# Routers in TensorE's column groups, and an earlier start of three mixture-of-experts stages

## The reference

```python
def moe_swiglu(u, router_w, w1, w3, w2):            # "MoE 1" here
    logits = (tokens @ router_w).astype(F32)        # 256 x 1024 by 1024 x 8
    top_vals, top_idx = lax.top_k(logits, TOP_K)
    gates = jax.nn.softmax(top_vals, axis=-1)
    ...                                             # tokens sorted by expert
    return (jax.nn.silu(xb @ w1[e]) * (xb @ w3[e])) @ w2[e]

def grouped_moe(x, router_w, router_b, w_gate, w_up, w_down):   # "MoE A", "MoE B"
    scores = jax.nn.sigmoid(xt @ router_w)          # 1024 x 16
    sel = scores + router_b
    group_score = lax.top_k(sel.reshape(-1, N_GROUPS, GROUP_SIZE), TOP_K)[0].sum(-1)
    top_group = jnp.argmax(group_score, axis=-1)
    _, idx = lax.top_k(jnp.where(in_group, sel, -jnp.inf), TOP_K)
    gate = gate / gate.sum(-1, keepdims=True)
    for e in range(N_EXPERTS_2):
        h = jax.nn.silu(xt @ w_gate[e]) * (xt @ w_up[e])
        out = out + combine[:, e:e + 1] * (h @ w_down[e])
```

## Time and profile before

| | |
|---|---|
| median of three runs | 2630.08 us |
| the profiled execution's own time | 2639.58 us |
| its span | 2637.7 us |
| TensorE busy | 2414.2 us (92%) |
| VectorE, ScalarE busy | 479.3 us, 358.8 us |
| mean DMA rate | 243 GB/s |

### The profile page before, as it was taken

The page is one execution under the profiler, slowest core; times in us unless marked ns, Lnnn a source line. Parts: engine busy times, 40 slices in busy tenths (PEclk is TensorE's granted clock), DMA queues, the critical chain, the costliest instruction groups (busy, mean ns, idle before and its releaser), DMA issues. The chain is left out here.

```text
span 2637.7 us, 34623 instructions
## 1 busy us (share of the span) xinstructions
PE 2414.2 (92%) x15312; PEld 1056.6 (40%) x15312; DVE 479.3 (18%) x1109; ACT 358.8 (14%) x847; POOL 33.5 (1%) x77
## 2 busy tenths in 40 slices
PE   4997877999899899999999999987899989789997
PEld 2574653444576433222222223254432228442222
DVE  2133342000248400000000000113100021210002
ACT  2013221000232110000000000021100011110000
POOL 2000000000000000000000000000000000000000
PEclk9998668999999899999999999987799999789999
DMA  8222145542463489999999999921799972359994
GB/s 282 96 96 96 64 168 194 192 160 100 167 248 141 153 292 322 366 367 365 363 365 365 365 366 364 326 82 61 250 360 365 365 283 80 113 195 364 364 360 154
DMA packets 446102, 644.54 MB, mean 244 GB/s; under 512 B 10723, under 2 KB 345019, under 8 KB 445947
## 3 DMA queue, kind: packets, MB, share of 16 engines
q1 hardware_dynamic: 442011, 629.55, 69.5%
q0 software_dynamic: 3936, 12.69, 1.5%
HBM read 641.15 MB, written 1.05 MB: 243 GB/s over the span
## 5 line engine op out<-in xcount | busy, mean ns | idle before, releaser
L1024 PE MATMUL bank<-ring,wide 128*32 128x512 f32 x7296 | 809.8, 596 | 2.6 <-issue 1.7
L1024 PEld LDWEIGHTS bank<-ring,wide 128*32 128x32 f32 x7296 | 231.5, 110 | 551.2 <-issue 551.2
L1052 PE MATMUL bank<-dreg,RB 128*32 128x512 f32 x3648 | 415.0, 595 | 0.0
L1582 ACT ACTIVATE SG<-bank 128x256 f32<-128x256 f32 x114 | 43.7, 384 | 1194.5 <-PE bank L1024 1194.5
L1052 PEld LDWEIGHTS bank<-dreg,RB 128*32 128x32 f32 x3648 | 106.9, 109 | 223.7 <-issue 223.7
L697 PE MATMUL bank<-wide,ring 128*128 128x256 f32 x832 | 180.9, 379 | 0.0
L697 PEld LDWEIGHTS bank<-wide,ring 128*128 128x128 f32 x832 | 158.1, 190 | 22.6 <-issue 1.4
L953 PE MATMUL bank<-ring,wide 128*128 128x512 f32 x352 | 156.9, 600 | 6.5 <-DMA ring<-in_l_ffn_w 6.5
L2282 DVE TENSOR_TENSOR H<-SG,bank 128x256 f32<-128x256 f32 x66 | 27.8, 421 | 722.7 <-ACT SG L1582 722.7
L687 PE MATMUL bank<-ring,wide 128*128 128x512 f32 x352 | 156.7, 605 | 2.3 <-DMA ring<-in_w_kv 2.3
L687 PE MATMUL bank<-ring,T 128*128 128x512 f32 x256 | 114.3, 607 | 1.4 <-ACT sm L1749 0.8
(11 more groups left out here) (371 smaller groups left out, 1466.4 us busy)
## 6 DMA issues: line engine op xcount, KB each, us to landing
ring<-in_l_moe_w SPq DMA_DIRECT2D x176, 1024.0 KB, 11.5
dreg<-in_l_moe_w SPq DMA_DIRECT2D x88, 1024.0 KB, 12.3
ring<-in_w_gate SPq DMA_DIRECT2D x64, 1024.0 KB, 11.3
ring<-in_w_up SPq DMA_DIRECT2D x64, 1024.0 KB, 13.5
dreg<-in_w_down SPq DMA_DIRECT2D x64, 1024.0 KB, 12.4
ring<-in_l_mod_w SPq DMA_DIRECT2D x24, 2048.0 KB, 8.0
ring<-in_l_ffn_w SPq DMA_DIRECT2D x22, 1024.0 KB, 10.3
ring<-in_l_w_in SPq DMA_DIRECT2D x7, 2048.0 KB, 9.0
```

What stands on the lines that cost most here:

```text
L1024: mm = pe.matmul(banks[r % 2][32 * g:32 * g + 32, :], xg[:, k, at:at + 32], ring[:, i % RING, k, :], start=k == 0, stop=k == KC - 1)
L1052: return pe.matmul(banks[4 + 2 * (b % 2) + h][32 * g:32 * g + 32, :], HQ[:, r % 4, j, 32 * q:32 * q + 32], dring[:, i % RING, j, h * NCH:( ...
L1582: act.activation(SG[:, r % 2, :], banks[r % 2][:, 0:FSTEP], ACT.Silu).then_inc(sem("moe_silued"), 1)
```

## The change

The change has five parts.

- **Router.** The router's weights are now the stationary operand: 32 columns (8 + 16 and 8 zero columns, `wrt` is widened), and all 256 tokens stream past. The 8 chunks go to the four column groups in two rounds, so PSUM holds four partial sums in four quarters of the partitions. ScalarE copies them to SBUF (`take_router`), and a second product by a stacked identity (`quad_sum`) adds the quarters and turns the result to tokens by experts. `quad_sum` is made once, by three small additions on VectorE ahead of the attention loop.
- **Bins ahead of the gates.** `choose` copies the mask to `chosen` as soon as it is known.
- **Places.** One triangle product covers both halves, one product by ones adds the first half's count; the totals go to a bank of their own (`cnt`), after the places are handed over. The numbers to compare with start at 1, so the step by -1 is gone.
- **One-hot halves.** Each half has a semaphore step; between the two VectorE takes the totals and frees their bank.
- **TOK.** The clearing (MoE 1) or scaling (A, B) of `TOK` is moved behind the one-hot matrix, as are MoE 1's gates.

```diff
+            def router(m, lo, n):
+                b, q = bank_of[f"part{m.name}"]
+                o = bank_for(f"part{m.name}")
+                for r in range(2):
+                    for g in range(4):
+                        k = 4 * r + g
+                        operand_chunk(k, True)
+                        i = pe.matmul(o[QUAD * g:QUAD * (g + 1), 0:T], wrt[:, k, :], T1[:, k, :], start=r == 0, stop=r == 1)
+                filled(i, f"part{m.name}")
+                o = bank_for(f"rt{m.name}")
+                pe.wait_ge(sem(f"bank_read{b}"), q + 1)
+                pe.wait_ge(sem("quad_sum_made"), 1)
                 for t in range(TT):
-                    for k in range(KC):
-                        m = pe.matmul(o[:, t * n:(t + 1) * n], T1[:, k, t * P:(t + 1) * P], wrt[:, k, lo:lo + n],
-                                      start=k == 0, stop=k == KC - 1)
+                    i = pe.matmul(o[:, t * n:(t + 1) * n], router_parts[:, t * P:(t + 1) * P], quad_sum[:, lo:lo + n], start=True, stop=True)
...
-                pe.matmul(o[:, 0:nb], upper, v[:, 0, :], start=True, stop=True)
-                pe.matmul(o[:, nb:2 * nb], upper, v[:, 1, :], start=True, stop=False)
-                pe.matmul(o[:, nb:2 * nb], ones, v[:, 0, :], start=False, stop=True)
+                pe.matmul(o[:, 0:2 * nb].rearrange("p (t b) -> p t b", t=TT), upper, v, start=True, stop=False)
+                filled(pe.matmul(o[:, nb:2 * nb], ones, v[:, 0, :], start=False, stop=True), f"pos{m.name}")
+                o = bank_for(f"cnt{m.name}")
                 for t in range(TT):
-                    i = pe.matmul(o[:, 2 * nb:3 * nb], ones, v[:, t, :], start=t == 0, stop=t == 1)
-                filled(i, name)
+                    i = pe.matmul(o[:, 0:nb], ones, v[:, t, :], start=t == 0, stop=t == 1)
+                filled(i, f"cnt{m.name}")
...
+                        if n == 0:
+                            upto("all_placed", t + 1)
                         i = pe.matmul(o[:, 0:half], src[:, t, k * P:(k + 1) * P], rhs, start=t == 0, stop=t == 1)
...
-                upto("all_placed", 1)
...
+            def take_router(m):
+                o = take(f"part{m.name}")
+                freed(act.activation(router_parts, o[:, 0:T], ACT.Copy), f"part{m.name}")
...
+            step(dve.tensor_tensor(quad_sum[:, :], ident[:, 0:QUAD], ident[:, QUAD:2 * QUAD], ALU.add))
+            step(dve.tensor_tensor(quad_sum[:, :], quad_sum[:, :], ident[:, 2 * QUAD:3 * QUAD], ALU.add))
+            step(dve.tensor_tensor(quad_sum[:, :], quad_sum[:, :], ident[:, 3 * QUAD:4 * QUAD], ALU.add), "quad_sum_made")
...
+                for t in range(TT):
+                    dve.tensor_tensor(PMG[:, t * 2 * half:(t + 1) * 2 * half]..., ALU.is_equal).then_inc(sem("moe_all_placed"), 1)
+                    if t == 0:
+                        o = take(f"cnt{m.name}")
+                        step(dve.reduce_max(sm[:, 300:301], o[:, 0:nb], axis=AX.X))
+                        free(dve.memset(junk, 0.0), f"cnt{m.name}")
```

More of the change, by code:

```diff
@@ L237, in two_blocks @@
         gbias = sb("gbias", [GR, 2])
-        wrt = sb("wrt", [P, KC, NE1 + NE2])
+        wrt = sb("wrt", [P, KC, QUAD])
+        quad_sum = sb("quad_sum", [P, QUAD])
         rbias = sb("rbias", [P, NE2])
@@ L561, in step @@
                 pool.wait_ge(sem(name), cnt[name])
+            step(pool.memset(wrt[:, :, NE1 + NE2:], 0.0))
             step(pool.memset(ident[:, :], 0.0))
@@ L1317, in _ @@
             turn_job(X)
-            router("rtA", NE1, NE2)
+            router(MOEA, NE1, NE2)
             places(MOEA)
@@ L1335, in _ @@
             turn_job(X)
-            router("rtB", NE1, NE2)
+            router(MOEB, NE1, NE2)
             places(MOEB)
@@ L1703, in _ @@
             copy_values(1, 1)
+            def take_router(m):
+                o = take(f"part{m.name}")
+                freed(act.activation(router_parts, o[:, 0:T], ACT.Copy), f"part{m.name}")
             operand(T1, SCL[:, 4, :], MODX[:, 1, 24:32])
+            take_router(MOE1)
             act.wait_ge(sem("router_max"), 1)
@@ L1752, in _ @@
             for l, name in ((0, "A"), (1, "B")):
+                take_router(MOEA if l == 0 else MOEB)
                 o = take(f"rt{name}")
@@ L2221, in ranks @@
                 step(dve.tensor_reduce(dst, s0, axis=AX.X, op=ALU.add))
-            dve.memset(TOK[:, :, :], 0.0)
             for f in GAP5:
@@ L2229, in _, with choose, sort_tokens @@
             ranks(R1, gates[:, :, 0:NE1])
+            def choose(m, mask):
+                step(dve.tensor_copy(chosen[:, :, 0:m.bins], mask), "bins_chosen")
+            def sort_tokens(m, mask):
+                nb = m.bins
+                o = take(f"pos{m.name}")
+                v = place[:, :, 0:nb]
+                step(dve.scalar_tensor_tensor(v, o[:, 0:2 * nb].rearrange("p (t b) -> p t b", t=TT), 1.0, mask, ALU.add, ALU.mult))
+                free(dve.memset(junk, 0.0), f"pos{m.name}")
+                half = 4 * CAP
+                wide_chunks = chunks[:, 0, :] if m is MOE1 else chunks[:, :, :].rearrange("p a n -> p (a n)")
+                n = 2 * half // m.bins
+                for t in range(TT):
+                    dve.tensor_tensor(PMG[:, t * 2 * half:(t + 1) * 2 * half].rearrange("p (b n) -> p b n", b=m.bins),
+                                      wide_chunks.rearrange("p (a n) -> p a n", a=1).broadcast_to([P, m.bins, n]),
+                                      place[:, t, 0:m.bins].rearrange("p (b a) -> p b a", a=1).broadcast_to([P, m.bins, n]),
+                                      ALU.is_equal).then_inc(sem("moe_all_placed"), 1)
+                    if t == 0:
+                        o = take(f"cnt{m.name}")
+                        step(dve.reduce_max(sm[:, 300:301], o[:, 0:nb], axis=AX.X))
+                        free(dve.memset(junk, 0.0), f"cnt{m.name}")
+                i = MOES.index(m)
+                step(dve.tensor_scalar(flag[:, i:i + 1], sm[:, 300:301], float(CAP), None, ALU.is_gt), "flag_ready")
             step(dve.tensor_scalar(sm[:, 208:224], sm[:, 208:224], 2.0, None, ALU.is_lt))
+            choose(MOE1, R1)
             step(dve.reduce_max(sm[:, 62:64], gates[:, :, 0:NE1], axis=AX.X))
             step(dve.tensor_scalar(sm[:, 60:62], sm[:, 62:64], -1.0, None, ALU.mult), "router_max")
+            sort_tokens(MOE1, R1)
+            dve.memset(TOK[:, :, :], 0.0)
             dve.wait_ge(sem("router_act"), 1)
@@ L2237, in _ @@
             for t in range(TT):
[L2238 to L2252 removed]
+                i = dve.tensor_scalar(gates[:, t, 0:NE1], gates[:, t, 0:NE1], sm[:, 62 + t:63 + t], None, ALU.mult)
+            step(i)
             def moe(m):
                 upto = lambda name, n: dve.wait_ge(sem(f"moe_{name}"), m.before[name] + n)
[L2257 to L2265 removed]
                 if m is not MOE1:
@@ L2436, in _ @@
                 projected(name, 8 if l == 0 else 11)
-                dve.tensor_scalar(TOK[:, :, :], X[:, :, :], ALPHA, None, ALU.mult)
                 group_router(name)
@@ L2440, in _ @@
                 sort_tokens(m, sm[:, 280:288].rearrange("p (t g) -> p t g", t=TT))
+                dve.tensor_scalar(TOK[:, :, :], X[:, :, :], ALPHA, None, ALU.mult)
                 moe(m)
```

56 lines of the change are left out of this document (16 added, 40 removed).

## The result

The changed kernel takes 2604.93 us (median of 4 runs, 2604.45 to 2605.75); the kernel before took 2632.78 in the same comparison (2628.11 to 2637.06). The ratio is 0.9886, 95% interval 0.9861 to 0.9910. The profiled execution took 2605.75 us with a span of 2604.0, where before's took 2639.58 and 2637.7.

What follows compares the result with a forecast made beforehand. The prediction held that TensorE's work bounds the expert rounds and dependent steps delay each gather. Earlier gathers 13.1 plus router 3.3 less added work 0.7 gave 15.7 us, from median 2630.08 to 2614.4 us, range 2607 to 2625.

Steps and rivals of the forecast that it cites:

- Bound: Whole kernel: TensorE's own work sets the expert rounds' length, stream close behind; dependent steps ahead of each gather delay everything after.
- rival 1: Weight stream is the bound, so MoE 1's earlier gather finds weights late: 8.6 us gain left, 2621.5; chance 0.10.
- Bins, places, one-hot halves: Chain from chosen bins to gather: starts 5.83, 3.63 and 3.61 us earlier in MoE 1, A, B; together 13.1 us.
- Rival 2: Change does half: first one-hot half doesn't release the gather, router gains nothing; 9.0 us gain, 2621; chance 0.10.
- Router: Column-group router ahead of the choice: results 1.3, 1.0 and 1.0 us earlier over three stages, 3.3 us in all.
- the bound of 4.5: Upper limit of the new router's summed gain, 4.5 us, with the full clock everywhere.
- `quad_sum`: Three dependent VectorE rows ahead of the attention loop cost 0.7 us, or 0 if the loop has that much play.
- The stream's rest: MoE 1's weight stream rests 5 us after about 938; a 7.1 us advance removes that, queueing at most 2 us.
- the clock's luck at the top: 2.5 us of favourable clock, counted in the upper end of the forecast's 11 to 20 us gain.
- rival 4: Less idle time raises the clock earlier in gather and slot gates, 2 us per stage: 20 to 22 us, 2609; chance 0.04.
- Rival 3: TensorE stays at its lower clock: gathers wholly there take 20.5 us, kernel 8 us slower, 2638; chance 0.04.
- Sum and range: Whole kernel: 13.1 + 3.3 - 0.7 = 15.7 us gain, likeliest 2614.4 us, range 2607 to 2625.

## Why the prediction was wrong in its size

- **Bound.** Right. Stage chains set the length, not the stream: rival 1 fell. The expert rounds kept their length, and all 7.4 us of MoE 1 reached the end of its rounds.
- **Bins, places, one-hot halves.** Right to 0.3 us. `chosen` (or its place) to gather: 5.84, 3.78 and 3.75 us earlier, 13.4 where 13.1 was forecast. The wait that takes the place of the removed one was there: the totals' bank. Rival 2 fell.
- **Router.** Mis-sized: 7.42 - 5.84, 5.44 - 3.78 and 5.62 - 3.75 are 1.6, 1.7 and 1.9, 5.1 us instead of 3.3, past the bound of 4.5. In A and B I had the sigmoid's table load wait for the second product, as it had waited for the router in the rows of before. It runs beside it: it starts 0.74 us ahead of where it would stand behind the product (1835.14 against 1835.81 + 0.07), and as much in B, 1.5 of the 1.8 us. With the lower clock on the old router there are 2.8 us more, which the bounds didn't hold at all.
- **`quad_sum`.** Its three rows stand at 227.35, 227.58 and 227.81 after, and the next row 0.68 us behind the first. The attention loop's first product came 0.7 us later, as forecast (10.98 us behind the transposes instead of 10.27), but from there the two traces scatter by 1 to 2 us in both directions. Whether the 0.7 reached the end isn't shown.
- **The stream's rest.** The ninth to twelfth loads are issued at 916.76, and the next at 932.64, 15.9 us apart instead of 23.5, so the advance was taken from the stream's rest, without a new wait of TensorE:

```profile
916.76 5.55 SPq L494 DMA_DIRECT2D dreg<-in_l_moe_w  x4
932.64 0.99 SPq L486 DMA_DIRECT2D ring<-in_l_moe_w  x2
```

- **The clock.** This is the step that failed: "2.5 for the clock's luck at the top", and rival 4 ("The clock rises earlier as well", 2 us in each stage) with a chance of 0.04. Placement was worth some 10 us between these two kernels (estimate above), 15 in the two profiled executions, and half of it lay in stretches that the change doesn't touch, ahead of MoE 1 and MoE B. I had looked for the clock only behind the shortened waits, and took the one profiled execution's placement for the kernel's. Without that term even the right chain, 18.5 - 0.7 = 17.8, gives 2630.08 - 17.8 = 2612.3 and not 2604.93.
- **Rival 4** came nearest: 2609 by its sum. Gathers, slot gates and first rounds of A and B gave 7.5 us by the clock, but MoE 1's gather gave nothing (12.49 us in both traces), and that the clock there rises because the waits are shorter isn't borne out: with one delay, and so longer waits, the kernel before was faster.
- **Rival 3** (slower, clock stays low) fell. It wanted gathers near 20.5 us; they took 12.46 to 12.76, and not above 13.5 in the delayed kernels. That a kernel can lose up to 9 us more than its chain they do show, by other stretches.
- **Sum and range.** `quad_sum` stands with 0.7 us in the sum and with 0.9 in rival 2 and at the bottom of the range. The range's own rule (9 to 20 us of gain, single runs 2 below and 5 above the median) gives 2608 to 2626 and not 2607 to 2625. Neither slip changes the account. The base of 2630.08 was low, if anything: the kernel before's median over 33 later runs is 2638.23.

The Trainium skill ("TensorE: Matmul & The Clock Gate", Part 1: The HAM clock gate) says that the same kernel sees the clock rise after differing counts of products and that "the ramp penalty is <1% of a typical kernel span". The runs agree with the first: the same gather of MoE 1 took 12.49 and 12.69 us in the two traces of the changed kernel. They don't agree with the second for this kernel: in the kernel before TensorE was busy for 212 us of its time at the lower clock, and if that work takes twice as long there it costs some 106 us (an estimate from the trace), 4% of the span. What differs of it between two versions, some 10 us, is 0.4%, and the change's own chain was worth 0.7%.

## What to carry to other kernels

Work out a chain of waits from rows, and most of its links come out to some tenths of a microsecond. But in a kernel whose TensorE falls to its lower clock in some two dozen stretches, two versions also differ by how these falls lie, here by about 5 us for each, and by 9 to 10 us beyond the chain between kernels that differ only in a needless delay. Put that spread into the range of any forecast, and before crediting a change (or dropping one) of this size, time both kernels with two or three small delays added as well, and compare the families. A change can also take work out of reach of the lower clock: the old router's 32 records took 3.8 to 4.1 us in A and B or 6.9, the new one's 16 took 1.4 to 1.9 in every trace. Such a change is worth more than its chain at one placement says.

## What the runs showed of the hardware

- The same instructions in the same order have a few distinct lengths rather than a spread, by the one trace of each kernel: memory attention ahead of MoE B took 118.6, 119.8 to 120.0, 122.4 to 122.5 or 123.3 us in seventeen kernels, the slot gates 5.3 to 5.9 or 7.6 to 8.1 and nothing between.
- Short products without a gap didn't keep the upper clock. Windows of the kernel before in MoE A, of the gather's end, the slot gates' start and their rest:

```profile
1865.70:1873.50 7.80, 7.80 (x27) 4.60 (x25) 0.00 (x0) 2.94 (x6) 0.00 (x0) 1.00 0.97 384
1873.50:1876.00 2.50, 2.50 (x25) 2.50 (x23) 0.00 (x0) 1.77 (x2) 0.00 (x0) 0.99 0.00 0
1876.00:1881.00 5.00, 5.00 (x25) 5.00 (x25) 0.00 (x0) 0.00 (x0) 0.00 (x0) 0.50 0.00 0
```

  TensorE is busy for all of it; in the last window, with products of 4 streamed columns in it and ahead of it, the clock is at 0.50. The changed kernel's slot gates in A run at 1.00 to their end at 1861.4, and the clock falls directly behind them: the window from 1861.4 to 1866.0 has a mean of 0.63.
- An ACT_TABLE_LOAD can run ahead of the wait of its ACTIVATE: 1835.14 to 1836.42, beside the product from 1835.22 to 1835.81 that the ACTIVATE reads. The ACTIVATE follows 0.01 behind the load. It need not: in every kernel with the old router the sigmoid's load stood behind the wait, and the square root's does so in the changed kernel too. ScalarE in the changed kernel with the old router, MoE A, and in the changed kernel itself:

```profile
1839.03 1.28 ACT L1763 ACT_TABLE_LOAD   x1 [3.01 <-PE bank L1225]
```

```profile
2268.63 1.28 ACT L1377 ACT_TABLE_LOAD   x1 [30.02 <-DVE sm L1855]
```

  What decides which of the two a load does stays open here; whoever forecasts a chain with one should price both. The Trainium skill ("ScalarE: Activation LUTs", What ACT_TABLE_LOAD costs) gives 1283 ns for the load, as here, and about 1.4 us more for a drain; no such drain shows here.
- The new router adds a change between column groups and the whole array in each stage. Its second product starts 0.10 us behind the end of ScalarE's copy in A (1835.22 less 1835.12), so no price of it is to be seen.
